# A two-layer decoder trunk: row copies for the dispatch products of the first two experts, filled pauses, row loads and one weight load moved

## The reference

```python
for layer in range(DEPTH):                       # DEPTH = 2
    mix = conformer_conv(...) if layer == 0 else swa_sink_attention(...)
    x = deepnorm(x, mix, ln_g[layer, 0], ln_b[layer, 0])
    ffn = grouped_moe(x, router_w, router_b, w_gate[layer], w_up[layer], w_down[layer])
    x = deepnorm(x, ffn, ln_g[layer, 1], ln_b[layer, 1])
# grouped_moe, per expert e: h = silu(xb @ w_gate[e]) * (xb @ w_up[e]);  y = h @ w_down[e]
```

## Time and profile before

| | us |
|---|---|
| median of 3 executions | 1109.61 |
| lowest and highest | 1108.69, 1113.83 |
| the profiled execution, its own time | 1114.09 |
| its span | 1112.4 |
| PE busy | 968.1 (87%) |
| DVE busy | 446.7 (40%) |
| POOL busy | 185.9 (17%) |
| ACT busy | 163.9 (15%) |
| bytes moved | 308.69 MB |

### The profile page before, as it was taken

One profiled execution on the slowest core, in us unless ns is written; L12 is line 12 of the kernel. 1 busy time (PEld: TensorE's weight loads), 2 busy tenths in 40 slices (PEclk: granted clock), 3 DMA queues, 4 the chain that ended last, 5 costly groups with the idle time before them and its releaser, 6 DMA issues.

```text
span 1112.4 us, 15368 instructions
## 1 busy us (share of the span) xinstructions
PE 968.1 (87%) x5930; PEld 521.7 (47%) x5930; DVE 446.7 (40%) x909; ACT 163.9 (15%) x384; POOL 185.9 (17%) x304
## 2 busy tenths in 40 slices
PE   7999989999996879987669899968997969898994
PEld 4444344567553434543434454534664534454541
DVE  4799953551110111110675556575411212121116
ACT  0000022301110001000222332433010000010100
POOL 1320020213202022200430001011221210303022
PEclk9999989889998999999779999987998989999997
DMA  9994399946999999999730004200699999999953
GB/s 301 383 410 152 86 342 372 405 165 234 384 385 384 422 372 394 392 407 402 246 148 1 1 1 148 79 1 4 255 371 359 387 382 425 379 412 376 410 209 113
DMA packets 74614, 308.69 MB, mean 277 GB/s; under 512 B 9423, under 2 KB 21627, under 8 KB 58010
## 3 DMA queue, kind: packets, MB, share of 16 engines
q1 hardware_dynamic: 35744, 227.43, 53.2%
q10 hardware_dynamic: 28794, 54.03, 13.1%
q0 software_dynamic: 9984, 25.97, 6.7%
HBM read 250.33 MB, written 53.74 MB: 273 GB/s over the span
## 4 chain that ended last, share of the span: by engine, by line
PE 43%; DMA 21%; issue 17%; DVE 13%; POOL 2%; ACT 1%; ACTq 1%; SPq 1%; POOLq 0%; DVEq 0%
PE ps L724 15%; DMA wring<-in_moe_w_up_dram 9%; DVE arena L1067 7%; PE ps L734 7%; PE ps L624 6%; DMA wring<-in_moe_w_gate_dram 5%; PE ps L683 3%; PE ps L744 3%; DMA arena<-xs_dram 2%; PE ps L923 2%; PE ps L754 1%; DMA wring<-in_conv_w_dram 1%; POOL rstd L1841 1%; SPq L438 1%; PE ps L521 1%
## 5 line engine op out<-in xcount | busy, mean ns | idle before, releaser
L724 PE MATMUL ps<-wring,arena 128*64 128x256 f32 x1536 | 186.4, 398 | 23.3 <-DMA wring<-in_moe_w_gate_dram 16.8
L724 PEld LDWEIGHTS ps<-wring,arena 128*64 128x64 f32 x1536 | 114.2, 143 | 90.0 <-DMA wring<-in_moe_w_gate_dram 20.6
L560 PE MATMUL ps<-arena,wring 128*128 128x512 f32 x256 | 110.4, 593 | 1.4 <-DVE arena L1025 1.4
L1271 DVE COPY arena<-ps 128x256 f32<-128x256 f32 x32 | 13.6, 425 | 221.9 <-PE ps L832 211.2
L1067 DVE SCALAR_TENSOR_TENSOR arena<-arena,dwT 128x512 f32<-128x512 f32 x145 | 100.0, 764 | 0.0
L1855 POOL DMA_DIRECT2D arena<-xs_dram x112 | 59.5, 538 | 206.4 <-DVE arena L1250 164.0
L902 PE MATMUL ps<-wring,arena 128*128 128x512 f32 x192 | 86.5, 606 | 3.5 <-ACT arena L1697 3.5
L734 PE MATMUL ps<-wring,arena 128*64 128x512 f32 x384 | 86.5, 592 | 0.6 <-DVE arena L1271 0.6
L560 PEld LDWEIGHTS ps<-arena,wring 128*128 128x128 f32 x256 | 48.5, 190 | 62.1 <-issue 60.3
L724 PE MATMUL ps<-arena 128*64 128x256 f32 x512 | 63.4, 404 | 13.0 <-DMA arena<-in_moe_w_gate_dram 6.9
L1841 POOL TENSOR_TENSOR rstd<-vareps,half 128x1 f32<-128x1 f32 x20 | 24.7, 1235 | 294.9 <-DVE vareps L1084 294.9
(11 more groups left out here) (231 smaller groups left out, 1078.1 us busy)
## 6 DMA issues: line engine op xcount, KB each, us to landing
wring<-in_moe_w_gate_dram SPq DMA_DIRECT2D x24, 2048.0 KB, 23.6
wring<-in_moe_w_up_dram SPq DMA_DIRECT2D x24, 2048.0 KB, 20.0
wring<-in_moe_w_down_dram SPq DMA_DIRECT2D x24, 2048.0 KB, 19.7
xs_dram<-zero ACTq DMA_DIRECT2D x2, 16384.0 KB, 50.5
arena<-in_moe_w_up_dram SPq DMA_DIRECT2D x8, 2048.0 KB, 23.3
arena<-in_moe_w_down_dram SPq DMA_DIRECT2D x8, 2048.0 KB, 25.8
arena<-in_moe_w_gate_dram SPq DMA_DIRECT2D x8, 2048.0 KB, 28.9
xs_dram<-arena ACTq DMA_DIRECT2D x60, 128.0 KB, 8.8
```

The lines of the kernel that those rows point to most:

```text
L560: last = pe.matmul(ps[:, 2 * (c % 4) + h, :], w[:, k, h, (c % 2) * P:(c % 2) * P + P], xT[:, k, :], start=(k == 0), stop=(k == KD - 1))
L724: mm = pe.matmul(ps[h * CAP:(h + 1) * CAP, bank, 0:256], act[:, k, :], w[:, k, h * 256:(h + 1) * 256], start=(k == 0), stop=(k == KD - 1))
```

## The change

1. **Permuted copies.** ScalarE copies every normed tile into x_perm[layer][t], where the eight slices stand one after the other, and the products read x_perm[l][t][:, k, :]. PE waits for the copy (s_xp). The copies lie in free parts of the arena, so GpSimd's gathers now wait for s_firstx, and a small array of `table` (cmpx) moves to another place.
2. **Pieces and pauses.** The pieces are 0 to 4, 5 to 7, 8 to 19, 20 to 23 and 24 to 31 in layer 0 (0 to 2, 3 to 6, 7 to 19, 20 to 23, 24 to 31 in layer 1). Eight identity transposes follow the third piece, four the fourth.
3. **Row loads.** attn_bo and the two rows of layer 1's first norm are loaded at the attention's start (s_rows3), the two of its second norm after the attention's first tile. bq and kv_b stay in the experts of layer 0 (experts 7 and 8).
4. **One weight.** Weight 7 of layer 1 is issued when all of layer 1's scatters have landed.

```diff
-        cmpx = view(AT, E, XBLK)
+        cmpx = kvrow[:, 288:288 + E * XBLK].rearrange("p (e n) -> p e n", e=E)
+        x_perm = [[view(2048, KD, P), view(3072, KD, P), view(AT, KD, P), xTt], [view(i * D, KD, P) for i in range(T)]]
@@ sync
-            for m in range(5, RING):
+            for m in range(5, RING - 1):
                 weights(1, m)
+            sp.wait_ge(s_scat, 16 * 2 * T * DEPTH)
+            weights(1, RING - 1)
@@ tensor
                     if k == 0 or i == begin:
+                        pe.wait_ge(s_xp, T * l + t + 1)
                         pe.wait_ge(s_first, T * l + t + 1)
-                    last = pe.matmul(..., x_sb[:, t, k::KD],
+                    last = pe.matmul(..., x_perm[l][t][:, k, :],
                                      firsts[:, t, :], start=False, ...)
-            first_products(0, 0, 4)
+            first_products(0, 0, 5)
             turn_d(T - 1)
-            first_products(0, 4, 7)
+            first_products(0, 5, 8)
             logits_d(T - 1)
-            first_products(0, 7, 19)
+            first_products(0, 8, 20)
+            idle(1, 8)
             stage_r(T - 1)
-            first_products(0, 19, T * KD)
+            first_products(0, 20, 24)
+            idle(1, 4)
+            first_products(0, 24, T * KD)
...
+                if u[0] in "ER" and u[1] == T - 1:
+                    idle(1, 8 if u[0] == "E" else 4)
+            first_products(1, 24, T * KD)
@@ scalar
+            def permuted(l, t):
+                act.wait_ge(s_ln, 2 * T * l + t + 1)
+                act.activation(x_perm[l][t], x_sb[:, t, :].rearrange("p (j k) -> p k j", k=KD), ACT.Copy).then_inc(s_xp, 1)
...
+                if t == T - 2:
+                    permuted(0, 0)
+                    permuted(0, 1)
+            permuted(0, T - 2)
             normed(T - 1)
+            permuted(0, T - 1)
...
-                    if l == 0 and 4 <= e < 9:
-                        attention_row(e - 4)
+                    if l == 0 and 7 <= e < 9:
+                        attention_row(e - 7)
...
+            act.dma_start(resrow, attn_bo[0].partition_broadcast(P)).then_inc(s_rows3, 16)
+            norm_rows(1, 0, s_rows3)
             for t in range(T):
...
+                if t == 0:
+                    act.wait_ge(s_ln, 2 * T)
+                    norm_rows(1, 1, s_rows2)
+            permuted(1, 0)
+            permuted(1, 1)
             for u in last_units:
                 take(u)
-            norm_rows(1, 1, s_rows2)
+                if u == ("E", T - 2):
+                    permuted(1, T - 2)
+            permuted(1, T - 1)
@@ gpsimd
                 pool.wait_ge(s_extra, l + 1)
+                pool.wait_ge(s_firstx, l + 1)
...
-            pool.wait_ge(s_rows1, 16 * 5)
+            pool.wait_ge(s_rows3, 16 * 3)
             own(pool.tensor_scalar(resrow, resrow, 1.0 / ALPHA, None, ALU.mult))
```

More of the change, by code:

```diff
@@ L247, in trunk @@
         s_rows2 = sem("s_rows2")
+        s_rows3 = sem("s_rows3")
         s_pool0 = sem("s_pool0")
@@ L326, in trunk @@
         s_firstx = sem("s_firstx")
+        s_xp = sem("s_xp")
         s_diag = sem("s_diag")
@@ L681, in first_products @@
                     if k == 0 or i == begin:
+                        pe.wait_ge(s_xp, T * l + t + 1)
                         pe.wait_ge(s_first, T * l + t + 1)
-                    last = pe.matmul(ps[:, FIRST_BANKS[l][k // 4], (k % 4) * P:(k % 4 + 1) * P], x_sb[:, t, k::KD],
+                    last = pe.matmul(ps[:, FIRST_BANKS[l][k // 4], (k % 4) * P:(k % 4 + 1) * P], x_perm[l][t][:, k, :],
                                      firsts[:, t, :], start=False, stop=(t == T - 1 and k % 4 == 3))
@@ L979, in values @@
                 last.then_inc(s_O, 1)
-            first_after = {("W1", T - 1): (0, 3), ("Db", T - 1): (3, 7), ("E", T - 1): (7, 19), ("R", T - 1): (19, T * KD)}
+            first_after = {("W1", T - 1): (0, 3), ("Db", T - 1): (3, 7), ("E", T - 1): (7, 20), ("R", T - 1): (20, 24)}
             pe.wait_ge(s_yg[0], 32)
@@ L1361, in _ @@
             dve.wait_ge(s_ropeT, 1)
-            dve.wait_ge(s_rows1, 16 * 5)
+            dve.wait_ge(s_rows1, 16 * 2)
             def rotate(t, src, heads, dst, tmp):
@@ L1377, in norm_tile @@
             def norm_tile(t, n):
+                if t == 0:
+                    dve.wait_ge(s_rows3, 16 * 3)
                 taken(dve, ("W0", t))
```

## The result

The change ran 12 times at a median of 1107.09 us (1098.91 to 1110.11) beside the kernel before at 1114.74 (12 runs, 1107.62 to 1121.84, the first three of them those of the table above). The ratio is **0.9927 [0.9902, 0.9952]**: about 8 us less, where 12.2 had been forecast. (The ratios in this document are those on record; the plain quotient of two medians differs from them by up to 0.2%, most for only_rows: 1.0001 against 0.9979.) 1107.09 lies above the forecast range, for two reasons: the gain was 4 us smaller, and the first three runs of before had a median 5.1 us under that of twelve. Either alone would not have put it there: 8.1 less than 1109.61 is 1101.5, and 12.2 less than 1114.74 is 1102.5. The profiled execution took 1105.96 us, with a span of 1104.3; its lines are those of the new kernel (products L689, gate and up L733, down L743, identity transposes L533).

A forecast was written before the change was run, and what follows sets the result against it. Both layers' experts were taken as bound by weight streams near 390 GB/s, attention and convolution by engine steps. 4.5 + 4.0 + 1.0 + 2.7 = 12.2 us off the 1109.6 median gave 1097.4, range 1090 to 1104.5.

The forecast's parts named there:

- Products of layer 0, 4.5 us: Layer 0's dispatch: adjacent-column loads and fills start expert 0 and the stream 4.5 us earlier, bounds 4.4 to 5.3.
- Rows out of layer 0's stream, 4.0 us: Layer 0's experts: three row loads, 1.57 MB, leave the weight stream, saving 4.0 us at 0.393.
- Attention, 1.0 us: Attention's start: moved row loads free VectorE, 1.5 us back less 0.5; net 1.0, bounds -1 and 1.5.
- same stall again: Attention: GpSimd's moved row work holds another VectorE step as long, with ACT's issues in the open; bound -1 us.
- Layer 1, 2.7 + 0: Layer 1's experts: two row loads, 1.05 MB, leave the stream, 2.7 us; earlier products and held weight 7 give 0.
- A: Layer 1 isn't bound by bytes and PE's time counts: 10.9 us more gained, 1086.5; chance 0.10.
- B: Layer 0's dispatch: the clock stays low longer despite the identity transposes; total gain some 9 us, 1100.5; chance 0.12.
- C: Layer 0's products: loads aren't sped, products stay at 0.241 us, fills add 1.3; 1103.2; chance 0.06.
- D: Layer 1: each us scatters land after 816 is lost; 1106.9 at 825.5; chance 0.08 up to 834, 0.04 beyond.

The follow-up runs named there:

- only_rows: The kernel before with part 3 alone, the five row loads moved; 1113.74 us, 0.9979 of the kernel before.
- only_products: The kernel before with parts 1 and 2 alone (permuted copies, pieces, fills); 1110.29 us, 0.9969 of the kernel before.
- strided: The change with products reading x_sb at stride 8 again, copies, waits and fills kept; 1110.42 us, 0.9962 of the kernel before.
- no_hold_again: Second measurement of the change without part 4, weight 7 not held; 1104.28 us, 0.9894 of the kernel before.
- hold_more: The change with weights 6 and 7 both waiting for the scatters; 1107.13 us, 0.9928 of the kernel before.
- hold_short: The change with weight 7 waiting for layer 1's last 0/1 product, not the scatters; 1101.59 us, 0.9873 of the kernel before.
- hold_short_again: Second measurement of hold_short, same edit on the change; 1103.25 us, 0.9907 of the kernel before.
- no_hold: The change without part 4, weight 7 issued with 5 and 6 again; 1102.55 us, 0.9891 of the kernel before.

## Why the prediction was right and wrong

**Products of layer 0, 4.5 us.** Loads 192 ns (190 said), expert 0 at 253.80 (255.7 said, with an execution that began its products 1.2 us earlier). The dispatch gave 6.8. The term was too small by the choice of the lower clock: I let 8 instructions, the fill and 16 more run at the 0.50 of the earlier trace rows, but with the faster products and the fills together the clock stayed at 1.00, and expert 0's first 96 products took 10.58 us besides, where they had taken 12.27 (before, timeline of PE):

```profile
260.12 12.27 PE L724 MATMUL ps<-wring,arena 128*64 128x256 f32 x96 [0.84 <-ACT arena L1652]
```

The range for the term, up to 5.3, left out this last piece. But the experts behind it take longer when they start earlier: with rows in the stream 255.0 (only_products) against 252.4 and 253.0, without them 248.6 and 248.0 with strided products against 250.9, the mean of the nine with copied rows. About 2.4 us are thus paid back, and 6.8 - 2.4 = 4.4 reach the end of the layer. The number was right there by luck, by two errors that cancel. Why the stream takes longer by that amount isn't settled; in the first ten us after the ring load it moves 296 to 324 GB/s in the kernels with copied rows and 342 to 354 in those with strided products, about 0.4 MB or 1 us.

**Rows out of layer 0's stream, 4.0 us.** From the same comparison: strided products 252.7 to 248.3, copied rows 255.0 to 250.9. 4.4 and 4.1 us. The term was right. From the first product to the layer's end the nine kernels with both take 272.9 us on average, the two with neither 281.0 and 280.0: about 8, and I had said 8 to 9.

**Attention, 1.0 us.** The mechanism was right and the sum wrong. The rotation step runs in 0.43 us, unheld (L1382, which answers to L1370 of the earlier trace rows):

```profile
561.00 0.43 DVE L1382 TENSOR_TENSOR arena<-arena,cosb 128x256 f32<-128x256 f32 x1
```

and the turns of the second tile of x begin 54.2 to 54.8 us after the attention's start in the kernels with the rows moved, 55.7 to 56.4 in the three without: 1.5 us, as counted. (In no_hold_again and hold_more a later rotation step takes 2.4 us instead, the lower bound's "same stall again".) A hundred us in, it is gone. Windows of before and of the change, each 95 us after its attention's start:

```profile
616.80:621.80 5.00, 4.08 (x21) 2.62 (x20) 2.81 (x5) 1.47 (x3) 0.00 (x0) 0.80 0.00 0
621.80:626.80 5.00, 5.00 (x13) 2.28 (x12) 1.61 (x4) 2.17 (x9) 0.00 (x0) 1.00 0.01 2
```

```profile
606.60:611.60 5.00, 4.11 (x13) 2.41 (x11) 2.85 (x5) 2.73 (x9) 0.00 (x0) 0.50 0.52 180
611.60:616.60 5.00, 5.00 (x11) 2.22 (x10) 1.56 (x3) 0.64 (x4) 0.00 (x0) 0.79 0.01 3
```

A granted clock of 0.80 over 5 us means the upper level from about 619 on, 97 us after the stage's start; in the change it rises at about 614, 102 us after it. The third and fourth turn of x lie 54.5 us apart there and 51.8 in before: 2.7 us lost. It isn't an effect of the rows: only_products, without them, shows it too (third and fourth turn 54.5 us apart), and hold_short, with them, has the clock of before and is 1.1 us shorter than before. Which of the two comes looks like a draw; what decides it stays open.

**Layer 1, 2.7 + 0.** This is where the step that failed lies: part 4, the hold of weight 7, set at 0, "the 2 us of a pause and as much in return". The pause came, 2.6 us, and nothing came in return. The hold alone makes the kernel before 0.46% slower [0.15, 0.77], some 5 us; in the changed kernel it costs 0.31%, 3.5 us, and the four measurements without the wait for the scatters have a mean ratio of 0.9891, which is 12.1 us under before: what had been forecast for the whole. So the other terms held on the whole, and the missing 4 us are, as far as these runs tell, those of the hold. That they add up so well is partly luck: the attention's 1.0 isn't there, and each of these numbers is uncertain by 2 us or more.

How the hold costs is open. A pause of 2 to 4 us in front of expert 2's rows or behind them stands in most traces, with the hold or without. PE's early arrival at expert 2 looks like what decides, since strided, with no gather's wait, has the shortest layer 1 but one (277.4); but hold_short_again waited 8.5 us there and took 277.2, and the change and hold_more waited 2.2 and 0 and took 280.8 and 281.0. Put as a sum, 277.5, plus 2.7 with the rows in the stream, plus the pause, meets the stages of the table within 1.6 us, except only_rows; but the 277.5 was fitted afterwards, and the pause itself is uncertain by 1 us.

A further cut of layer 1, at the end of expert 7's down products, says more. Up to there the four traces with the rows in the stream take 148.7 (before), 152.8, 152.2 and 152.7 us, the ten without them 143.7 to 149.8. The trace of before is the short one of its kind by 3.5 to 4 us, and this is one reason why layer 1 seems to have given nothing beside it. From there to the end it is 130.0 to 134.0 us in thirteen traces and 140.4 in only_rows. So the 288.6 of only_rows isn't a matter of its bytes: it reached the cut after 148.2 us, as before did, and lost 9 behind it, in part at the lower clock and in waits for rows of later experts (window and timelines of PE and DVE):

```profile
945.00:958.00 13.00, 8.55 (x91) 3.85 (x83) 1.35 (x3) 0.76 (x2) 2.02 (x4) 0.74 1.02 343
```

```profile
1011.85 3.66 PE L745 MATMUL ps<-wring,arena 128*32 128x256 f32 x64 [3.07 <-DVE arena L1281]
```

```profile
1011.15 0.64 DVE L1281 STREAM_TRANSPOSE arena<-arena 128x256 f32<-128x256 f32 x1 [4.37 <-DMA arena<-xs_dram]
```

**Rivals.** A (layer 1 keeps its gains) is refuted: only_products, with the faster products in layer 1 too, needs 284.1 us there and not 5 less than 279.9. B (low clock) and C (loads not faster) are refuted by the windows and by strided. D named the right place, the hold of weight 7, and it came in small: by its rule 1 us for the 1 us by which the scatters landed later than estimated. The stream lost more, since weights 5 and 6 were through 2 us before them; I had added the scatters' bytes to the weights' and so put both ends at 816.

**The total** of the two profiled executions is 12.2 - 1.0 - 2.7 for the two steps that gave nothing there, less the 0.9 and 1.1 us by which these stages grew, plus 0.5 in layer 0 (9.0 against 8.5): 7.0, and 1.2 by accident before the dispatch. What took the time out of the range as well was the level: three runs of before for a median.

## What to carry to other kernels

A stationary operand of 128 float32 columns took 336 ns to load with a stride of 8 and 192 with adjacent columns; a copy on an engine that was idle paid for itself. What a faster step brings is decided by the next thing that it meets: an earlier consumer in front of a ring of weights can stop the stream it was waiting for, and a load held back leaves a hole unless something else is ready to move: the step that I had set at 0 cost the 4 us that were missing. Where the edits are worth single us each, cut the spans at fixed events and compare stages, but take more than one execution of each kernel: repeats differed by up to 3.7 us in a stage. And forecast a ratio or take the level from many runs.

## What the runs showed of the hardware that I had not expected

ScalarE pays for a stride as TensorE's loads do: a copy of 128x1024 float32 takes 2.06 us with the strided read of L1600 and 1.06 with adjacent elements.

Executions of the same code differ by 4 us ahead of anything that the change makes faster, and the clock goes with it: the first product of layer 0 comes at 235.8 to 236.3 us in seven of the fourteen traces and at 239.5 to 240.7 in the other seven, with nothing between. In the first seven the granted clock rises again at 158.5 to 159.5 us in the convolution, in the others at 164.1 to 167.0. Windows of the change and of no_hold, in the convolution:

```profile
155.00:160.00 5.00, 4.77 (x22) 4.44 (x22) 1.30 (x4) 2.76 (x8) 0.00 (x0) 0.50 0.99 360
160.00:165.00 5.00, 5.00 (x9) 2.46 (x9) 2.07 (x5) 0.13 (x1) 0.55 (x1) 0.50 1.03 404
165.00:170.00 5.00, 5.00 (x11) 2.19 (x10) 0.00 (x0) 0.00 (x0) 0.00 (x0) 0.85 1.05 410
```

```profile
155.00:160.00 5.00, 4.58 (x24) 4.15 (x24) 1.48 (x4) 2.90 (x8) 0.00 (x0) 0.66 1.03 391
160.00:165.00 5.00, 4.95 (x12) 2.32 (x13) 1.94 (x5) 0.00 (x0) 0.55 (x1) 1.00 0.98 382
```

In the same stretch the clock stays at its lower level for over 11 us in the one and for about 3 in the other. Together with the same kind of draw in the attention that is 6 to 7 us, a good part of the 9 to 14 us between the fastest and the slowest of twelve runs, and three runs of before can well lie 5 us under the median of twelve.
